# Latent attention of the prompt with keys and values per head, fewer rows and columns a product, and unread products moved

## What is computed

```python
q_lat = jnp.einsum('bshn,chn->bshc', q_nope, w_uk)          # 64 numbers a head -> 128
s = einsum('bqhc,bkc->bhqk', q_lat, ckv) + einsum('bqhr,bkr->bhqk', q_rope, kr)
p = softmax(where(mask, s * 96 ** -0.5, NEG_INF))
ctx = einsum('bhqk,bkc->bqhc', p, ckv)                       # 128 numbers a head
o = jnp.einsum('bqhc,chv->bqhv', ctx, w_uv).reshape(...) @ w_out   # 128 -> 64 a head
```

## Time and profile before

| | us |
|---|---|
| median of 3 runs | 1028.42 |
| lowest, highest | 1027.04, 1034.55 |
| profiled execution, first to last instruction | 1029.5 |
| latent stage, blocks of prompt attention | 644.2 to 704.9 |
| page attention | 704.9 to 735.1 |

### The profile page before, as it was taken

How to read it: one execution, slowest core, us unless ns; L and a number is a source line. 1 busy time by engine, 2 the same in 40 slices (tenths; PEclk the granted TensorE clock), 3 DMA queues, 4 the chain that set the end, 5 groups by cost and what they waited for, 6 DMA issues and landing times.

```text
span 1029.5 us, 17722 instructions
## 1 busy us (share of the span) xinstructions
PE 964.9 (94%) x6944; PEld 596.7 (58%) x6944; DVE 512.0 (50%) x1071; ACT 357.9 (35%) x894; POOL 246.0 (24%) x291
## 2 busy tenths in 40 slices
PE   7999999998998998899999998999899979999995
PEld 6876787888444856433334766657648654333332
DVE  0245530376748678333222555784188783323227
ACT  3335532020001534234333353655214542443323
POOL 3550000052500012555210016400000025552130
PEclk9999999999999998899999999999999987999998
DMA  9836101172206166899999504441237166999977
GB/s 319 193 108 227 42 1 34 49 205 82 72 0 172 43 283 220 293 353 418 412 418 397 195 22 99 90 155 42 74 132 286 42 241 206 351 415 414 417 210 179
DMA packets 78060, 203.61 MB, mean 198 GB/s; under 512 B 19128, under 2 KB 44384, under 8 KB 68880
## 3 DMA queue, kind: packets, MB, share of 16 engines
q1 hardware_dynamic: 61568, 153.44, 40.8%
q0 software_dynamic: 16400, 48.93, 15.3%
HBM read 184.46 MB, written 25.92 MB: 204 GB/s over the span
## 4 chain that ended last, share of the span: by engine, by line
PE 73%; DVE 13%; DMA 6%; ACT 4%; issue 3%; POOL 1%; SPq 0%; DVEq 0%; POOLq 0%; ACTq 0%
PE PS L1658 15%; PE PS L1445 10%; PE PS L1088 9%; PE PS L1675 7%; PE PS L1192 6%; PE PS L1476 3%; DMA x<-y_tok 2%; PE PS L1646 2%; ACT arena L2064 2%; PE PS L1111 2%; DMA arena<-in_moe_w_in_dram 2%; PE PS L1916 2%; PE PS L1072 1%; PE PS L1906 1%; PE PS L1153 1%
## 5 line engine op out<-in xcount | busy, mean ns | idle before, releaser
L1658 PE MATMUL PS<-ring,arena 128*32 128x512 f32 x696 | 137.6, 592 | 0.5 <-DMA arena<-in_moe_w_in_dram 0.5
L2064 ACT ACTIVATE arena<-PS 32x520 f32<-32x520 f32 (+9 forms) x155 | 76.7, 505 | 176.1 <-PE PS L1088 43.0
L1658 PE MATMUL PS<-arena 128*32 128x512 f32 x600 | 108.4, 605 | 2.0 <-issue 2.0
L1088 PE MATMUL PS<-xT,ring 128*128 128x260 f32 x416 | 95.2, 390 | 4.3 <-DVE arena L2566 3.1
L3154 DVE COPY arena<-PS 128x256 f32<-128x256 f32 x24 | 10.2, 425 | 173.6 <-PE PS L1666 173.6
L1088 PEld LDWEIGHTS PS<-xT,ring 128*128 128x128 f32 x416 | 79.5, 193 | 19.1 <-DVE arena L2566 5.1
L2363 ACT ACTIVATE arena<-PS,lnc 128x128 f32<-128x128 f32 x184 | 66.9, 468 | 38.0 <-PE PS L1646 38.0
L1658 PEld LDWEIGHTS PS<-ring,arena 128*32 128x32 f32 x696 | 37.1, 110 | 55.1 <-issue 50.2
L848 POOL TENSOR_TENSOR rstd<-rstd,small 128x1 f32<-128x1 f32 (+1 forms) x20 | 13.5, 675 | 225.2 <-DVE rstd L2854 225.2
L1675 PE MATMUL PS<-ring,arena 128*32 128x512 f32 x408 | 65.4, 595 | 0.6 <-DVE arena L3154 0.6
L1192 PE MATMUL PS<-ring,xT 128*128 128x256 f32 (+2 forms) x336 | 65.2, 354 | 0.0
(11 more groups left out here) (444 smaller groups left out, 1833.7 us busy)
## 6 DMA issues: line engine op xcount, KB each, us to landing
ring<-in_moe_w_in_dram SPq DMA_DIRECT2D x29, 1024.0 KB, 11.7
arena<-in_moe_w_in_dram SPq DMA_DIRECT2D x25, 1024.0 KB, 10.5
ring<-in_moe_w_out_dram SPq DMA_DIRECT2D x17, 1024.0 KB, 11.4
ring<-in_w_in_even_dram SPq DMA_DIRECT2D x11, 1024.0 KB, 12.3
xT<-in_moe_w_in_dram SPq DMA_DIRECT2D x10, 1024.0 KB, 11.5
arena<-in_moe_w_out_dram SPq DMA_DIRECT2D x9, 1024.0 KB, 11.0
xT<-in_moe_w_out_dram SPq DMA_DIRECT2D x6, 1024.0 KB, 13.7
y_tok<-in_c_zeros_dram POOLq DMA_DIRECT2D x8, 512.0 KB, 11.1
```

The costliest lines, as they stand in the source:

```text
L1088: mm = pe.matmul(o[out_rows, 512 * h:512 * h + HALF], lhs(k), rhs(k)[:, HALF * h:HALF * h + HALF], start=(k == 0), stop=(k == nk - 1))
L1658: mm = pe.matmul(o[group(q), 0:512], xT_[:, k, group(q)], w(q, k), start=(k == 0), stop=(k == KD - 1), **quarter(q))
L2064: return act.activation(dst, src, ACT.Copy)
```

## The change

Keys and values per head are computed for the prompt: "kn" (`head_keys`) makes 64 key numbers a head and "vt" (`head_values`) 64 value numbers a head from the latent rows of 512 tokens. Scores then multiply queries of 64 numbers, and outputs have 64 numbers and go straight to oT. The samples keep the latent form; their part of "ql" becomes one step of 8 small products behind score 1, with the rotary transposes of the samples, and "uv" becomes one step for the 8 sample columns. The unread products around the last rotary transposes go; there are three each ahead of qrT 2 and 3, and 4, 3, 1 or 0 ahead of each turn of blocks with 1, 2, 3 or 4 key tiles. Of the ten gain and bias operations four follow blocks 12 to 15 and six stand in the page attention. The rotary rows of the pages get a place of their own.

```diff
-    out = [("S", 0), ("S", 1)]
+    out = [("S", 0), ("S", 1), ("samples", 0)]
...
-PAGE_DVE = keys("""pcT.0 pcT.2 pcT.4 max.0 pcT.7 scale.0 max.1 scale.1""")
-GAIN_BLOCKS = 6
+PAGE_DVE = keys("""pcT.0 pcT.2 pcT.4 max.0 pcT.7 scale.0 ga.2.0 ga.2.1 max.1 ga.3.0 scale.1 ga.3.1 ga.4.0 ga.4.1""")
+LATENT_GAINS = {12: (0, 0), 13: (0, 1), 14: (1, 0), 15: (1, 1)}
+LATENT_UNREAD = [4, 3, 1, 0]
...
+                       qn.1 qn.3 kn.1 qrT.0 vt.0 qrT.1 vt.1 qrT.2 qrT.3""")
...
-             ("oin", 3), ("oinT", 2), ("oin", 4), ("ukT",), ("qn", 0), ("oinT", 3), ("qn", 1), ("oinT", 4)]
+             ("oin", 3), ("oinT", 2), ("oin", 4), ("ukT",), ("qn", 0), ("oinT", 3), ("kn", 0), ("oinT", 4), ("qn", 1)]
+
+LATENT_JOBS = [key for key in LATENT_PE if key[0] != "oi2" and key not in (("qn", 0), ("oinT", 3), ("kn", 0), ("oinT", 4), ("qn", 1))]
+LATENT_JOBS += [("oinT", 3), ("qn", 0), ("oinT", 4), ("kn", 0), ("qn", 1)]
+LATENT_QUERIES = keys("""qn.2 qn.3 qrope.0 kn.1 qrope.1 qrT.0 vt.0 qrope.2 qrT.1 vt.1 qrope.3 qrT.2 qrope.4 qrT.3""")
...
+            for s, i in latent_steps(len(MLA_BLOCKS)):
+                jobs += [("ql",), ("qrT", 4)] if s == "samples" else [("mla" + s, i)]
             jobs += [("pkT", 0), ("pkT", 1), ("pN",)] + [key for key in PAGE_PE if key[0] != "row"]
-            jobs += [("uv", j) for j in range(4)]
+            jobs += [("uv",)]
...
-            piece(("uk",), io["w_uk"][0].rearrange("c h n -> c (h n)"), (512,), ("ukT",))
+            piece(("uk",), io["w_uk"][0].rearrange("c h n -> c (h n)"), (512,), ("kn", 1))
...
-        q_lat = part(8, T)
-        ctxT = q_lat
+        knT = part(4, SEQ)
+        natr = part(2 * D)
+        ctx_s = part(8, DB)
...
-        natr = x_flat[:, 0:2 * D]
...
+        v_at = 4 * T
+        v_lat = x_flat[:, v_at:v_at + 2 * D].rearrange("p (t n) -> p t n", t=4)
...
+                    if kind == "mla":
+                        unread_products(o[:, 896:1024], LATENT_UNREAD[blocks[i][0]])
...
+                def head_keys(i):
+
+                    key = ("kn", i)
+                    o = open_(key)
+                    landed(pe, ("uk",))
+                    taken(pe, ("oinT", 3))
+                    for j in range(2):
+                        c = 2 * i + j
+                        mm = pe.matmul(o[:, 512 * j:512 * j + SEQ], wview(("uk",))[:, c * P:c * P + P], ckvT[:, 0:SEQ], start=True, stop=True)
+                    close(mm, key)
...
+                def head_values(i):
+
+                    key = ("vt", i)
+                    o = open_(key)
+                    landed(pe, ("uv",))
+                    for j in range(2):
+                        mm = pe.matmul(o[:, 512 * j:512 * j + 512], ckvT[:, tile_cols(2 * i + j)], wview(("uv",))[:, :], start=True, stop=True)
+                    close(mm, key)
...
-                    if t == 4:
-                        unread_products(o[:, 896:1024], 10)
+                    if t in (2, 3):
+                        unread_products(o[:, 896:1024], 3)
...
-                q_rope(0)
-                taken(pe, ("ukT",))
-                taken(pe, ("qn", 2))
-                taken(pe, ("qn", 3))
-                for h in range(8):
-                    key = ("ql", h)
-                    open_(key)
-                    b, c = 64 * (h % 2), h // 2
-                    close(by_feature(key, lambda k: ukT[b:b + 64, c, :], lambda k: qnT[b:b + 64, c, :], 1), key)
-                for t in range(1, NT):
-                    q_rope(t)
-                    q_rope_back(t - 1)
-                q_rope_back(4)
-                unread_products(pair(("qrT", 4))[:, 896:1024], 6)
-                taken(pe, ("qrT", 4))
-                taken(pe, ("ql", 6))
-                taken(pe, ("ql", 7))
+                steps = {"qn": query_chunk, "qrope": q_rope, "qrT": q_rope_back, "kn": head_keys, "vt": head_values}
+                for key in LATENT_QUERIES:
+                    steps[key[0]](*key[1:])
+
+                def sample_latents(_):
+
+                    key = ("ql",)
+                    o = open_(key)
+                    taken(pe, ("ukT",))
+                    for h in range(8):
+                        b, c = 64 * (h % 2), h // 2
+                        mm = pe.matmul(o[:, 512 * (h % 2) + DB * c:512 * (h % 2) + DB * c + DB], ukT[b:b + 64, c, :], qnT[b:b + 64, c, 512:520], start=True, stop=True)
+                    close(mm, key)
+                    q_rope_back(4)
+
+                for key in (("kn", 0), ("kn", 1)) + tuple(("qn", j) for j in range(4)):
+                    taken(pe, key)
...
+                    taken(pe, ("qrT", n))
                     for h in range(h0, h0 + g):
-                        pe.matmul(o[:, h - h0, 0:w], q_lat[:, h, n * P:n * P + P], ckvT[:, 0:w], start=True, stop=False)
+                        b, c = 64 * (h % 2), h // 2
+                        pe.matmul(o[:, h - h0, 0:w], qnT[b:b + 64, c, n * P:n * P + P], knT[b:b + 64, c, 0:w], start=True, stop=False)
...
+                    taken(pe, ("vt", n // 2))
                     for c in range(n + 1):
-                        mm = pe.matmul(o[:, 0:g * P], rows[:, c, 0:P], v[:, c, :, :], start=(c == 0), stop=(c == n))
+                        for h in range(h0, h0 + g):
+                            b = 64 * (h % 2)
+                            mm = pe.matmul(o[b:b + 64, 0:P], v_lat[:, c, 64 * h:64 * h + 64], v[:, c, h - h0, :], start=(c == 0), stop=(c == n))
...
-                landed(pe, ("uv",))
-                for j in range(4):
-                    key = ("uv", j)
-                    open_(key)
-                    for q in range(2):
-                        h = 2 * j + q
-                        mm = by_feature(key, lambda k: wview(("uv",))[:, 64 * h:64 * h + 64], lambda k: ctxT[:, h, :], 1,
-                                        out_rows=slice(64 * q, 64 * q + 64))
-                    close(mm, key)
+                key = ("uv",)
+                o = open_(key)
+                for h in range(8):
+                    b, c = 64 * (h % 2), h // 2
+                    mm = pe.matmul(o[b:b + 64, DB * c:DB * c + DB], wview(("uv",))[:, 64 * h:64 * h + 64], ctx_s[:, h, :], start=True, stop=True)
+                close(mm, key)
...
-                        take(att_key(kind, "O", i), ctxT[:, h0:h0 + g, tile_cols(n)],
-                             lambda o: o[:, 0:g * P].rearrange("p (g q) -> p g q", g=g))
+                        take(att_key(kind, "O", i), oT[:, h0 // 2, tile_cols(n)], lambda o: o[:, 0:P])
...
-                act.activation(st[0:1, 26:27], small[0:1, EPSILON:EPSILON + 1], ACT.Exp)
-                act.wait_ge(s["moe_done"], 1)
-                for j in (1, 3):
-                    take(("qn", j), halves(qnT[:, j, :]), halves)
-                for h in (1, 3, 5, 7):
-                    take(("ql", h), halves(q_lat[:, h, :]), halves)
-                for t in range(4):
-                    take(("qrT", t), qrT2[:, :, tile_cols(t)], lambda o: o[:, 0:256].rearrange("p (c q) -> p c q", c=2))
-
-                taken(act, ("ql", 6))
-                taken(act, ("ql", 7))
-                act.wait_ge(s["qrS_zero"], 1)
-                copy(qlS[:, :, 0:8], q_lat[:, :, 512:520].rearrange("p h b -> p b h"))
-                full(act, ("qrT", 4))
-                for q in range(4):
-                    ins = copy(qrS[32 * q:32 * q + 32, q, :, 0:8], pair(("qrT", 4))[32 * q:32 * q + 32, 0:64].rearrange("p (h b) -> p b h", h=8))
-                free(ins, ("qrT", 4))
-
-                act.wait_ge(s["moe_done"], 1)
-                latent_blocks()
+                    if key == ("oinT", 4):
+                        act.activation(st[0:1, 26:27], small[0:1, EPSILON:EPSILON + 1], ACT.Exp)
+                        act.wait_ge(s["moe_done"], 1)
+
+                def samples():
+                    act.wait_ge(s["qrS_zero"], 1)
+                    full(act, ("ql",))
+                    for par in range(2):
+                        ins = copy(qlS[:, :, par:8:2], pair(("ql",))[:, 512 * par:512 * par + 32].rearrange("p (c b) -> p b c", c=4))
+                    free(ins, ("ql",))
+                    full(act, ("qrT", 4))
+                    for q in range(4):
+                        ins = copy(qrS[32 * q:32 * q + 32, q, :, 0:8], pair(("qrT", 4))[32 * q:32 * q + 32, 0:64].rearrange("p (h b) -> p b h", h=8))
+                    free(ins, ("qrT", 4))
+
+                latent_blocks(samples)
...
-                    take(("uv", j), halves(oT[:, j, :]), halves)
+                take(("uv",), oT[:, 0:4, 512:520], lambda o: o[:, 0:32].rearrange("p (c b) -> p c b", c=4))
...
+                    if i in LATENT_GAINS:
+                        latent_gains(*LATENT_GAINS[i])
...
+                take(("kn", 0), knT[:, 0:2, :], pair(("kn", 0)).rearrange("p (c q) -> p c q", c=2))
                 for j in (0, 2):
                     take(("qn", j), halves(qnT[:, j, :]), halves(pair(("qn", j))))
-                rotate(0)
-                for h in (0, 2, 4, 6):
```

(27 more changed lines are left out.)

53 lines of the change are left out of this document (19 added, 34 removed).

## The result

The changed kernel takes 1023.73 us in the median of 20 runs, the kernel before 1029.84 in the median of 20 runs beside it. The ratio is 0.9931, with a 95% interval of 0.9911 to 0.995, so the gain is 7.1 us (5.1 to 9.2). They are not quotients of the medians, and differ from these by up to 0.005; where that matters, the quotient is given too. The forecast was a gain of 9.7 and a time of 1018.7. The time measured is 5.0 above that: 1.4 because the kernel before itself is slower in 20 runs than in the three first ones (1029.84 against 1028.42), 2.6 because the gain is smaller, and 1.0 from the difference between medians and ratio. The range went to 1024.0, so the time lies just inside its upper end.

A forecast was written before the change was run, and what follows sets the result against it. TensorE was taken to bound the kernel. -4.2 ahead of the blocks, -2.1 in them and -3.4 after the pages made -9.7 us: 1019.8 against the profiled span, 1018.7 against the median; range 1014.0 to 1024.0.

The forecast's parts named there:

- the second rival: At turn 0 or ahead of the projection the clock falls at a new gap, 1.9 us each: 1020.6 to 1022.5; chance 0.22.
- signs named beforehand: Right: first score about 640.2, last output 698 to 699, projection about 730; wrong: score of 1.7, clock under 1 near 645 or 730.
- Ahead of the blocks: Before the first score: latent queries and unread products go, key and value steps come, low clock ends; -4.2 us.
- Scores: In the 16 blocks, two heads' 64-row products overlap in two row halves: 17.2 us becomes 11.8, saving 5.4.
- Outputs: In the 16 blocks, two heads of 64 output rows lie side by side: 17.3 us becomes 11.9, saving 5.4.
- Unread products: 32 ahead of the blocks' turns, behind the PSUM wait, so they fill no wait and are charged whole: +7.1 us.
- The sample's step: In the blocks, 16 tiny products at 0.57 us and rotary transposes at 0.59: +1.2 us.
- Idle time: TensorE idle in the blocks, with turn 0 waiting for ScalarE: 2.6 us instead of 2.2, +0.4.
- VectorE: It keeps step in the last four blocks, and six scalings fit in the page attention: cost nothing.
- the rival that it bounds the last blocks: VectorE bounds the last four blocks and a scaling misses its gap: +0.5 us x 4, or 1020.7; chance 0.06.
- After the pages: Ahead of the output projection, 16 tiny products and one copy replace four value steps and a copy: -3.4 us.
- the rival that later loads stay where they are: In the experts, DMA engines are nearly full and loads do not move: up to 5 us given back, 1023.7; chance 0.03.

The follow-up runs named there:

- the run with a full clock and no gap: Changed kernel with the sample's copies behind the second exponentials, four scalings at blocks 3, 5, 7, 9, and unread products in waits ahead of the projection: 1020.28 us, ratio 0.9908.
- the same edits: Changed kernel with the sample's copies behind the second exponentials and six unread products in waits ahead of the projection, scalings left at blocks 12 to 15: 1017.88 us, ratio 0.9856.

## Why the prediction was right or wrong

Right in the amount of work, wrong in the clock at two places: the second rival, and not the forecast, is what happened. Of the signs named beforehand, the scores (1.06), the outputs (1.02) and the first score (639.54) came as for a right forecast; the last output (to 700.5) and the projection (731.95) came about 2 us late, with a low clock near 645 and 732, the sign of a wrong one. In the order of the prediction's steps, by the profiled executions:

- **Ahead of the blocks,** -4.2 forecast: the first score is at 639.54 instead of 644.39, -4.85, of which 0.36 was there at 606 us already, ahead of anything that the change touches. The key step took 1.95 in its gap, the 28 query instructions 6.52, and the clock of that stretch is 1.00. Right.
- **Scores,** 11.8 forecast: 0.42, 0.63, 0.85 and 1.06 for one to four key tiles, four times each, is 11.8. **Outputs,** 11.9: 0.37, 0.59, 0.81 and 1.02 make 11.2. That they overlap, and are not merely shorter, is shown for the scores (1.91 without). For the outputs it was not tried.
- **Unread products,** +7.1: 1.09 for four at full clock, less 0.2 because the turn behind them then takes 0.22 instead of 0.44. The charge was right, and the reading behind it ("nothing left for the products to fill") as well. What I missed is their effect: without them the clock is low for 23 to 36 us. I had counted 16 such products as removed ahead of the blocks and 32 as added, and never asked what either did to the clock.
- **The sample's step,** +1.2: 0.99 + 0.60 = 1.6. The 64-row products of 8 columns took 0.99 where those I took for their like take 0.57.
- **Idle time,** 2.6: 2.5. The wait of the first turn for ScalarE was found, about a microsecond (0.98). The step at which the forecast fails is beside it: the sum charges that wait and puts the clock of the blocks at nothing, without a reason. Only the second rival has it, at 0.22. Measured, 6.32 us at 0.52 are 3.0 us of lost full-clock work. The rival had the place right and the size too small (1.9); its reason, a new gap, isn't needed, as the clock also fell without a gap and ahead of one. Take these 3.0 off and the stage is 57.9, 2.5 below before, against the forecast 2.1; the run with a full clock and no gap gives 56.85.
- **VectorE,** 0: the rival that it bounds the last blocks falls (4.0 us a block with or without scalings). The wait at turn 14 (1.07 us) is in the idle time above.
- **After the pages,** -3.4: 0.94 instead of 4.47, -3.5. The page attention itself is 0.2 longer (30.52 against 30.31).
- **The projection,** 0: 15.53 us up to the first transpose behind it instead of 13.84, +1.7, at a clock of 0.66 for five microseconds. This too stands at nothing in the sum; the rival had 1.9 for it.

The sum up to there is -4.85 + 0.5 - 3.5 + 0.2 + 1.7 = -6.0, and the transposes behind the first part of the projection are 5.99 us earlier (747.48 instead of 753.47). The last long group of products, in the experts, is 5.63 us earlier (997.63, before 1003.26), so an earlier start did move the rest, through 110 us with the DMA engines nearly full: the rival that later loads stay where they are falls. The other 2.4 us of the profile's 8.1 are in the last 26 us. The chain of waits of the kernel before ends with

```profile
1008.38 5.42 issue
...
1013.81 7.67 DMA x<-y_tok
```

and that of the changed kernel has no such piece:

```profile
1001.79 0.28 issue
1002.07 7.34 DMA x<-y_tok
```

From the start of that last group to the end it takes 23.8 us in the changed kernel and 23.6 to 24.7 in the experiments, in the profile before 26.2. None of the edited code runs there, but with one profile of the kernel before, the cause of those 2.4 us stays open. Every run on record takes 1.6 to 1.9 us more than its span. So the profiled execution of before took about 1031.2 us, some 1.4 above its median of 20 runs, while that of the changed kernel took 1023.17, 0.6 below its own. These 2.0 us are the difference between the 8.1 of the two profiles and the 6.1 of the medians, with which the 6.0 of the stages agree.

The clocks of all runs agree. The median goes from 0.974 to 0.972, and 0.002 is 1.7 to 1.9 us; the gain was 2.6 short of the forecast. Rival 2, with one or two falls of the clock at 1.9 each, gave a gain of 5.9 to 7.8, and 7.1 lies in it. I had priced a fall at the one seen at 622 us; at the first turn it cost 3.0. That the time still came within the stated range owes something to luck: the start (-4.85 for -4.2) and the outputs (11.2 for 11.9) were 1.4 us better than forecast.

What stays open: what decides between low and full clock in one and the same order of work; whether small products are the cause; and whether the same edits are worth 1.4% (1.2% by the medians) on other chips.

## What to carry to other kernels

Price a product that nobody reads twice: once as TensorE time, and once by the clock of the stretch that it stands in, which the windows show; here 7 us of such products gave back at least about what they cost. When a change makes TensorE's products smaller (half the rows, 8 columns), reckon with a fall of the clock there even with TensorE never idle, and look for the place ahead of the long full-size products that follow. Compare the mean clock of all runs, not only of the profile: 0.01 of it was 8 to 10 us in this kernel, as much as the whole change.

## What the runs showed of the hardware

- The granted clock stayed at 0.50 for 36 us in which TensorE was recorded busy all the time, with products of 64 and 32 rows, 64 output columns and 128-column transposes. With 32 full 128x128 products more at the turns it was 1.00 throughout the stage in one of nine profiled executions and low for 3 to 14 us in the other eight.
- Two 64-row products in the two row halves overlap 1.8 times (1.91 against 1.06 for 512 columns). With 8 columns nothing is gained: sixteen 64-row instructions of 8 columns took 0.99 us, sixteen of 128 rows and 4 columns 0.57.
- A fall of the clock cost 3.0 us at the first turn and 1.7 at the projection, and the one at the projection came in one of two profiled executions of the same kernel. In 19 runs of it, between 1017 and 1031 us, the mean clock went from 0.979 to 0.963.
